# One core, two fused blocks: the first norm's factor applied where results leave PSUM, x loaded in four chunks and turned unnormalised, parameter rows on ScalarE's queue

## The chip, the cores and the metric

The kernel runs on one core of one Trainium2 chip. The metric is the device time of one execution in microseconds (us). Engines: PE (TensorE), ACT (ScalarE), DVE (VectorE), POOL (GpSimd), SP (SyncE, which issues most of the loads).

## The reference

`x` is 1 x 256 x 2048 (fp32). Two blocks follow each other; the change is in the first.

```python
h = rmsnorm(x, norm_mix_pre)                       # x * rsqrt(mean(x*x) + eps) * gain
proj = h @ w_in                                    # 2048 -> 2048 xr | 2048 yr | 2048 q | 256 k | 256 v | 2048 g_rnn | 2048 g_attn
xr = causal_depthwise_conv(xr, conv_w, conv_b)     # width 4
xr = rg_lru(xr, ...)                               # gates by two block matmuls, then a scan over the 256 positions
y_rnn = xr * gelu(yr)
q, k = rope(q), rope(k)
y_att = sliding_window_sink_attention(q, k, v, attn_sinks)
mix = sigmoid(g_rnn) * (y_rnn @ w_rnn_proj) + sigmoid(g_attn) * (y_att @ w_attn_proj)
x = x + rmsnorm(mix @ w_out, norm_mix_post)
# then an MLP with squared relu, and the whole second block (differential attention beside an S5 branch)
```

## The kernel before

**Work.** Every large product is done in fp32 by three matmuls: a weight tile is split into a rounded high part (`w_hi`, ACT, L639) and a low remainder (`w_lo`, DVE, L1079), the activations likewise (`h_hi`, `h_lo`). A *unit* is 512 output columns over all 2048 rows of a weight matrix: eight *subgroups* of 256 rows, each 512 KB of weights, 2 k-tiles, 12 matmuls of 512 columns (24 of 256 where the result is wanted feature-major). The weights of a subgroup pass through a ring of four buffers: SP loads `raw` (L362), ACT writes `w_hi`, DVE writes `w_lo`, PE multiplies. `split_hi` of subgroup g waits until PE has done all subgroups up to g-4; the load of subgroup g waits until DVE has split g-4. `LEAD` is 3: the loop index j of `steps` splits subgroup j+3 of the unit, so the last three turns of a unit prepare the next one. Everything else an engine does is hung between two such splits, as `hooks` by turn number. Each engine's order is written out by hand, and engines meet at semaphores.

**Order of units.** k and v (one unit, `U_KV`); then q and xr alternately, four of each; four units of yr; then 16 units of the mix, and so on. Results go to `acc[0]` and `acc[1]` in turn.

**Start.** SP issues x as one load of 2 MB, then 12 loads of parameter rows into `stg` (L353), then weights. When all 12 have landed PE transposes the two row tiles, and ACT copies them out as columns (`pt1`, `pt2`). Meanwhile ACT squares x (L664), DVE makes the mean square (L1109), POOL the factor `rstd` (L468). Then, for each of four chunks of 512 columns, in turn: ACT scales x by `rstd` into `stg` (L677), PE transposes it (L1745), ACT writes `h_hi` with the gain (L657), DVE `h_lo` (L1098). All four chunks use the same PSUM tile, so one chunk's turning waits for the one before. After POOL's first factor come its loads of gate weights: `load_rg(0)` at once, `load_rg(1)` when the last chunk has been scaled.

**Side work in the first units.** DVE: `rotary_angles`, `cosines_and_lambda`, `softplus`; ACT: `rotary_sines`, `exponentials`, each a hook in the k/v unit. Behind that unit ACT copies v out and DVE rotates k (L1204 and what follows).

**xr, yr and the recurrence.** At the first turn after an xr unit ACT copies `acc[0]` to `slab_d` (`xr_out`, L752), where POOL's convolution reads it. At the end of each yr unit ACT applies gelu straight from PSUM (L812), after it has waited for the convolution of that chunk. Beside yr unit c+1 runs the recurrence of chunk c, in turns of the same splits: PE's gate matmuls `rg(c)` (L1835), ACT `gates` (turn 2), `decays` (turn 3), `root` (turn 4), `y_high` (L772, turn 7); DVE `decay` (turn 3), `states` (turn 5, with the scan L1296), `y_product` (L1302, turn 6), `y_low` (L1307, turn 7).

The code that the change touches, with the line numbers of the profile:

Of the kernel before, what the change touches and what calls it, by code (L numbers as in the profile page):

```python
# [94 lines left out]
def griffin_block_then_ssm_block(nc, a, inv_freq, out):  # L95
    with ExitStack() as ctx:
# [107 lines left out]
        y_hi_ready = sem("y_hi_ready")  # L204
# [134 lines left out]
        def _(sp):  # L339
            x_in = a["x"][0].rearrange("(t p) d -> p t d", p=P)  # L340
            x_view = slab_i[:, :, :].rearrange("p (t k) c -> p t (k c)", t=TT)
            sp.dma_start(x_view, x_in).then_inc(x_landed, 16)
            for rows, tile in ((FIRST_ROWS, 0), (SECOND_ROWS, 1)):
                at = 0
                for name, n in rows:
                    src = a[name]
                    if name == "conv_w":
                        src = src[0].rearrange("w (r c) -> (w r) c", c=P)
                    elif len(src.shape) == 3:
                        src = src[0].rearrange("(r g) s -> r (g s)", g=2)  # L350
# [21 lines left out]
            unit(w_in, slice(o_k, o_k + NC), U_KV * S)  # L372
# [46 lines left out]
        def _(pool):  # L419
# [46 lines left out]
            for n in range(5):  # L466
                pool.wait_ge(ms_ready, n + 1)
                pool.tensor_tensor(small[:, 6:8], small[:, 4:6], neg_half[:, 0:2], ALU.pow).then_inc(rstd_ready, 1)  # L468
                if n == 0:
# [41 lines left out]
                    pool.wait_ge(stg_ready, NH)  # L511
# [115 lines left out]
        def _(act):  # L627
# [34 lines left out]
            act.wait_ge(x_landed, 16)  # L662
            for t in range(TT):
                ins = nc.scalar.activation(slab_d[:, 8 * t:8 * t + 8, :].rearrange("p k c -> p (k c)"), x_tok[:, t, :], ACT.Square,  # L664
                                           accum_out=ssq[:, t, 0:1])
            ins.then_inc(sq_ready, 1)

            act.wait_ge(pt_ready, 1)
            nc.scalar.activation(pt1[:, :], tps[:, 0:P], ACT.Copy)
            nc.scalar.activation(pt2[:, :], tps[:, P:2 * P], ACT.Copy).then_inc(cols_ready, 1)  # L670

            def h_chunk(c, t0, col):

                if c:
                    act.wait_ge(tps_ready, t0 + c)
                for t in range(TT):
                    ins = nc.scalar.activation(stg[:, t, :], x_tok[:, t, c * NC:(c + 1) * NC], ACT.Copy,  # L677
                                               scale=rstd[:, t:t + 1])
                ins.then_inc(stg_ready, 1)
                evac_hi(h_hi[:, c * QPC:(c + 1) * QPC, :], t0 + c + 1, col[:, c * QPC:(c + 1) * QPC])  # L680

            def first_unit(t0, const, col, hooks=None):

                for c in range(NH):
                    if c >= 2:
                        steps(None, 0, const, hooks, c - 1, start=c - 2)
                    h_chunk(c, t0, col)
                steps(None, 0, const, hooks, start=2)
# [13 lines left out]
            for j in range(LEAD):  # L702
                split_hi(None, 0, 0, j)


            act.wait_ge(rstd_ready, 1)
            first_unit(0, U_KV * S, pt1[:, COL1["norm_mix_pre"]:COL1["norm_mix_pre"] + KT],
                       {3: [rotary_sines], 5: [exponentials]})
            unit_over(None, 0, U_KV * S)
            nc.scalar.activation(v_tok[:, :, :], tok(acc[0])[:, :, SEQ:2 * SEQ], ACT.Copy).then_inc(v_ready, 1)  # L710
# [38 lines left out]
            def xr_out(i, c):  # L749
                unit_over(i, 2 * S, (U_QX + 1 + 2 * c) * S)  # L750
                settle()
                nc.scalar.activation(slab_d[:, span(i, QPC, QPC * c, QPC), :], feat(acc[0]), ACT.Copy).then_inc(acc_free[0], 1)  # L752

# [4 lines left out]
            steps(None, 0, U_QX * S, {5: [k_copy]})  # L758
            with act.Fori(0, NH - 1) as i:
                beside_xr, beside_q = attention(i, 0)  # L760
                steps(i, 2 * S, (U_QX + 1) * S, beside_xr)
                beside_q[0] = [lambda: xr_out(i, 0)] + beside_q.get(0, [])
# [3 lines left out]
            beside_yr[0] = [lambda: xr_out(None, NH - 1)] + beside_yr.get(0, [])  # L766
# [47 lines left out]


            def mix_unit(i, c, n, hooks=None):
                u = U_MIX + 4 * c + n
                steps(i, 4 * S, u * S, hooks)
                if n % 2 == 0:
# [5 lines left out]
                    nc.scalar.activation(tmp[:, :, :], tok(acc[u % 2]), ACT.Tanh, scale=0.5).then_inc(acc_free[u % 2], 1)  # L825
# [28 lines left out]

            def x_high(c, t0, col):


                act.wait_ge(tps_ready, t0 + c + 1)
                for b in range(QPC):
                    at = c * QPC + b  # L860
                    ins = nc.scalar.activation(h_hi[:, at, :], x_bank(c, b), ACT.Copy, scale=col[:, at:at + 1])
                ins.then_inc(tps_hi, 1)

            def x_squares(c, first_x):
                act.wait_ge(x_new, first_x + c + 1)
                for t in range(TT):
                    ins = nc.scalar.activation(e_tok[:, t, c * NC:(c + 1) * NC], x_tok[:, t, c * NC:(c + 1) * NC],
                                               ACT.Square, accum_out=ssq[:, t, c:c + 1])
                if c == NH - 1:
                    ins.then_inc(sq_ready, 1)  # L870
# [57 lines left out]
            act.wait_ge(row_ready, 1)  # L928
            nc.scalar.activation(row[:, :], side[0][:, 0:SEQ], ACT.Copy).then_inc(row_copied, 1)
# [143 lines left out]
        def _(dve):  # L1073
# [46 lines left out]
            mean_square(1, 1)  # L1120
            for j in range(LEAD):
                split_lo(None, 0, 0, j)

            def first_unit(hi_index, const, col, hooks=None):

                for c in range(NH):
                    if c >= 2:
                        steps(None, 0, const, hooks, c - 1, start=c - 2)
                    at = slice(c * QPC, (c + 1) * QPC)
                    evac_lo(h_hi[:, at, :], h_lo[:, at, :], hi_index + c, col[:, at])  # L1130
                steps(None, 0, const, hooks, start=2)
# [893 lines left out]
```

## Time and profile before

| | us |
|---|---|
| median of 3 runs | 2401.95 (2401.73 to 2402.02) |
| the profiled execution, its own time | 2403.9 |
| the profiled execution, its span | 2402.2 |
| PE busy in the span | 2269.6 (94%) |
| DVE / ACT / POOL busy | 1463.5 (61%) / 1192.6 (50%) / 457.7 (19%) |
| mean granted TensorE clock | 0.982 of full |

A timeline row reads: start and length in us, engine and line, operation, output from input, shapes, how many were merged; in brackets the idle time just before it and what ended it. The text uses *subgroup* numbers counted from the k/v unit's first: 0 to 7 are k/v, 8 to 15 the first q unit.

### The profile page before, as it was taken

What the parts mean: (1) busy time and instruction counts of PE and PEld (TensorE: products, weight loads), DVE (VectorE), ACT (ScalarE), POOL (GpSimd) and SP (SyncE); (2) the same over time, 40 slices, a digit from 0 to 9 for tenths busy, and PEclk for the clock granted to TensorE, in tenths of its full rate; (3) what the DMA queues carried; (4) which work ended last, traced back from release to release, by engine and by line L of the source; (5) the groups of instructions that cost most, each with busy time, mean ns of one, the idle gap of its engine ahead of it and who ended that gap; (6) DMA issues with size and microseconds to landing.
All of it is one profiled execution on the core that took longest, in us unless ns stands there. A gap on an engine that the chain in (4) does not pass through costs nothing.

```text
span 2402.2 us, 33351 instructions
## 1 busy us (share of the span) xinstructions
PE 2269.6 (94%) x11622; PEld 1902.4 (79%) x11622; DVE 1463.5 (61%) x1634; ACT 1192.6 (50%) x1804; POOL 457.7 (19%) x460
## 2 busy tenths in 40 slices
PE   4999999999999979999999999989999898989999
PEld 3888988788888768888888888869866686767887
DVE  3656669644554565555555555565998966665554
ACT  5455556644444445555555555554444444453443
POOL 2011385000000101211221121110656620100000
PEclk9999999999999989999999999999999999999999
DMA  6544444566666836666666666655555544445665
GB/s 184 176 149 144 145 123 150 172 189 193 190 188 195 261 117 198 200 207 198 198 206 196 200 206 196 199 172 176 171 171 172 179 149 141 147 133 169 183 193 165
DMA packets 214167, 426.41 MB, mean 178 GB/s; under 512 B 13984, under 2 KB 14272, under 8 KB 213312
## 3 DMA queue, kind: packets, MB, share of 16 engines
q1 hardware_dynamic: 206336, 398.64, 54.2%
q0 software_dynamic: 7744, 26.62, 3.4%
q8 instruction: 54, 0.88, 0.1%
q14 instruction: 33, 0.27, 0.0%
HBM read 414.71 MB, written 10.49 MB: 177 GB/s over the span
## 4 chain that ended last, share of the span: by engine, by line
PE 73%; DVE 11%; issue 8%; POOL 3%; ACT 3%; DMA 1%; SPq 0%; DVEq 0%; ACTq 0%; POOLq 0%
PE acc L1730 20%; PE acc L1732 20%; PE acc L1731 20%; DVE w_lo L1079 3%; PE acc L1722 3%; PE acc L1724 3%; PE acc L1725 3%; PE tps L1745 1%; POOL slab_f_f L567 1%; ACT w_hi L639 1%; DMA raw<-in_w_out_dram 1%; DVE k_t L1531 1%; POOL slab_f_f L568 1%; PE sides L1785 1%; PE tps L1803 1%
## 5 line engine op out<-in xcount | busy, mean ns | idle before, releaser
L1079 DVE TENSOR_TENSOR w_lo<-raw,w_hi 128x1024 fp32r<-128x1024 f32 x752 | 967.2, 1293 | 780.1 <-ACT w_hi L639 775.3
L639 ACT ACTIVATE w_hi<-raw 128x1024 fp32r<-128x1024 f32 x752 | 793.0, 1059 | 933.9 <-PE acc L1732 768.9
L1730 PE MATMUL acc<-w_hi,h_hi 128*128 128x512 f32 x1440 | 578.9, 402 | 20.5 <-DVE w_lo L1079 8.3
L1731 PE MATMUL acc<-w_lo,h_hi 128*128 128x512 f32 x1440 | 566.8, 394 | 0.0
L1732 PE MATMUL acc<-w_hi,h_lo 128*128 128x512 f32 x1440 | 566.4, 393 | 0.0
L1730 PEld LDWEIGHTS acc<-w_hi,h_hi 128*128 128x128 f32 x1440 | 274.5, 191 | 92.9 <-issue 23.7
L1732 PEld LDWEIGHTS acc<-w_hi,h_lo 128*128 128x128 f32 x1440 | 274.1, 190 | 59.1
L1731 PEld LDWEIGHTS acc<-w_lo,h_hi 128*128 128x128 f32 x1440 | 274.9, 191 | 54.1
L1730 PE MATMUL acc<-w_hi,slab_dg_r 128*128 128x512 f32 x768 | 300.2, 391 | 3.2 <-DVE w_lo L1079 3.2
L1732 PE MATMUL acc<-w_hi,slab_dg_r 128*128 128x512 f32 x768 | 299.5, 390 | 0.0
L1731 PE MATMUL acc<-w_lo,slab_dg_r 128*128 128x512 f32 x768 | 299.4, 390 | 0.0
L1722 PE MATMUL acc<-h_hi,w_hi 128*128 128x256 f32 x768 | 223.7, 291 | 8.9 <-DVE w_lo L1079 8.9
L1724 PE MATMUL acc<-h_lo,w_hi 128*128 128x256 f32 x768 | 219.2, 285 | 0.0
L1725 PE MATMUL acc<-h_hi,w_lo 128*128 128x256 f32 x768 | 219.1, 285 | 0.0
L1730 PEld LDWEIGHTS acc<-w_hi,slab_dg_r 128*128 128x128 f32 x768 | 144.5, 188 | 33.3 <-issue 3.5
L1732 PEld LDWEIGHTS acc<-w_hi,slab_dg_r 128*128 128x128 f32 x768 | 144.6, 188 | 30.2
L1731 PEld LDWEIGHTS acc<-w_lo,slab_dg_r 128*128 128x128 f32 x768 | 144.6, 188 | 30.0
L1722 PEld LDWEIGHTS acc<-h_hi,w_hi 128*128 128x128 f32 x768 | 149.0, 194 | 15.8 <-DVE w_lo L1079 10.0
L1724 PEld LDWEIGHTS acc<-h_lo,w_hi 128*128 128x128 f32 x768 | 149.3, 194 | 0.2
L1725 PEld LDWEIGHTS acc<-h_hi,w_lo 128*128 128x128 f32 x768 | 149.0, 194 | 0.0
L462 POOL DMA_DIRECT2D trig_scratch<-tmp x32 | 18.8, 589 | 447.3 <-DVE tmp L1454 433.2
L1730 PE MATMUL acc<-w_hi,slab_f_r 128*128 128x512 f32 x256 | 100.4, 392 | 0.0
(374 smaller groups left out, 2439.5 us busy)
## 6 DMA issues: line engine op xcount, KB each, us to landing
raw<-in_w_in_dram SPq DMA_DIRECT2D x328, 512.0 KB, 3.8
raw<-in_w_mlp_up_dram SPq DMA_DIRECT2D x128, 512.0 KB, 3.7
raw<-in_w_mlp_down_dram SPq DMA_DIRECT2D x128, 512.0 KB, 4.6
raw<-in_w_out_dram SPq DMA_DIRECT2D x64, 512.0 KB, 4.6
raw<-in_w_rnn_proj_dram SPq DMA_DIRECT2D x32, 512.0 KB, 3.9
raw<-in_w_attn_proj_dram SPq DMA_DIRECT2D x32, 512.0 KB, 4.6
trig_scratch<-tmp POOLq DMA_DIRECT2D x32, 256.0 KB, 4.0
raw<-in_w_proj_ssm_dram SPq DMA_DIRECT2D x16, 512.0 KB, 5.5
```

The costliest lines, as they stand in the source:

```text
L567: pool.tensor_tensor(xs[n % 4][:, 0, :], t2[:, 0, :], t1[:, 1, :], ALU.subtract).then_inc(state_ready, 1)
L568: pool.tensor_tensor(xs[n % 4][:, 1, :], t2[:, 1, :], t1[:, 0, :], ALU.add).then_inc(state_ready, 1)
L639: nc.scalar.activation(w_hi[:, j % RING], raw[:, j % RING], ACT.Copy).then_inc(hi_ready, 1)
L1079: V.tensor_tensor(w_lo[:, j % RING], raw[:, j % RING], w_hi[:, j % RING].bitcast(F32), ALU.subtract)\
L1531: chain.mark(V.tensor_tensor_scan(t1[:, 0, :], decay, t1[:, 0, :], 0.0, ALU.mult, ALU.add))
L1722: T.matmul(o, wh[:, c], hi[:, k, :], start=first and m % 2 == 0, stop=False, skip_group_check=True)
L1724: T.matmul(o, wh[:, c], lo[:, k, :], start=False, stop=False, skip_group_check=True)
L1725: ins = T.matmul(o, wl[:, c], hi[:, k, :], start=False, stop=last, skip_group_check=True)
L1730: T.matmul(o, hi[:, k, c], wh, start=first, stop=False)
L1731: T.matmul(o, hi[:, k, c], wl, start=False, stop=False)
L1732: ins = T.matmul(o, lo[:, k, c], wh, start=False, stop=last)
L1745: ins = T.transpose(tps[:, b * SEQ + t * P:b * SEQ + (t + 1) * P], stg[:, t, b * P:(b + 1) * P], ident[:, :])
```

## The change

x is loaded in four column chunks, with the weight loads of subgroups 0 to 2 between them. The parameter rows are issued by ACT, the five that are needed first counted apart from the other seven; the second tile is turned after subgroup 2. x is transposed as it is (`turn_x`, in `tps` and `sides` by turns), `h_hi` and `h_lo` get the gain only. The squares are taken beside the k/v unit (turns 1 to 4), the mean square at DVE's turn 5. `rstd` then enters where the results leave PSUM: in the v copy, in the cosines and sines (so in q and k), in the tanh scale of the mix gates, and, as a row over the features made by PE and copied by ACT (`row`), in the outputs of xr and yr. Those two are now multiplied by DVE; gelu follows on ACT from SBUF at turn 0 of the next unit. `exponentials` and `softplus` move to the first q unit; POOL's first `load_rg` comes with the later `rstd`.

```diff
@@ SP
-            sp.dma_start(x_view, x_in).then_inc(x_landed, 16)
-            for rows, tile in ((FIRST_ROWS, 0), (SECOND_ROWS, 1)):
...
-            unit(w_in, slice(o_k, o_k + NC), U_KV * S)
+            for c in range(NH):
+                at = slice(c * NC, (c + 1) * NC)
+                sp.dma_start(x_view[:, :, at], x_in[:, :, at]).then_inc(x_landed[c], 16)
+                if c < LEAD:
+                    load(w_in, slice(o_k, o_k + NC), 2 * c, U_KV * S + c, c)
+            for s in range(LEAD, S):
+                load(w_in, slice(o_k, o_k + NC), 2 * s, U_KV * S + s, s)
@@ POOL
-                    pool.wait_ge(stg_ready, NH)
+                    pool.wait_ge(tps_ready, NH)
                     load_rg(1)
@@ ACT
+            for rows, tile in ((FIRST_ROWS, 0), (SECOND_ROWS, 1)):
...
+                    act.dma_start(stg[at:at + n, tile, 0:P], src).then_inc(rows_landed[tile], 16)
...
+            pt_copy_(0)
+            act.wait_ge(cols_ready, 1)
+            x_high(0, 0, mix_gain)
+            split_hi(None, 0, 0, 0)
+            split_hi(None, 0, 0, 1)
+            x_high(1, 0, mix_gain)
+            split_hi(None, 0, 0, 2)
+            hooks = {s: [lambda c=s - 1: x_squares(c, None)] for s in range(1, 5)}
+            hooks[2].append(lambda: pt_copy_(1))
+            hooks[5] = [rotary_sines]
+            for c in range(2, NH):
+                x_high(c, 0, mix_gain)
+                steps(None, 0, U_KV * S, hooks, c - 1, start=c - 2)
+            steps(None, 0, U_KV * S, hooks, start=2)
+            unit_over(None, 0, U_KV * S)
             act.wait_ge(rstd_ready, 1)
...
+            for t in range(TT):
+                ins = nc.scalar.activation(v_tok[:, t, :], tok(acc[0])[:, t, SEQ:2 * SEQ], ACT.Copy, scale=rstd[:, t:t + 1])
...
-            steps(None, 0, U_QX * S, {5: [k_copy]})
+            steps(None, 0, U_QX * S, {1: [exponentials], 3: [lambda: row_copy(1)], 5: [k_copy]})
...
+            def gelu(c):
+                u = U_YR + c
+                act.wait_ge(acc_free[u % 2], u // 2 + 1)
+                at = slice(c * QPC, (c + 1) * QPC)
+                nc.scalar.activation(slab_d[:, at, :], slab_d[:, at, :], ACT.Gelu_apprx_tanh).then_inc(gelu_ready, 1)
...
-                return {2: [lambda: gates(c)], 3: [lambda: decays(c)], 4: [lambda: root(c)], 7: [lambda: y_high(c)]}
+                return {0: [lambda: gelu(c)], 2: [lambda: gates(c)], 3: [lambda: decays(c)], 4: [lambda: root(c)], 7: [lambda: y_high(c)]}
...
-                act.wait_ge(conv_ready, c + 1)
-                unit_over(None, 0, u * S)
-                nc.scalar.activation(slab_d[:, c * QPC:(c + 1) * QPC, :], feat(acc[u % 2]), ACT.Gelu_apprx_tanh)\
-                    .then_inc(acc_free[u % 2], 1)
@@ DVE
+                dve.wait_ge(rstd_ready, 1)
+                chain.mark(V.tensor_scalar(half_rstd, rstd, 0.5, None, ALU.mult))
+                for t in range(TT):
+                    for b in (cosb, sinb):
+                        chain.mark(V.tensor_scalar(b[:, t, :], b[:, t, :], rstd[:, t:t + 1], None, ALU.mult))
...
+            x_low(0, H_X, mix_gain)
+            split_lo(None, 0, 0, 0)
+            split_lo(None, 0, 0, 1)
+            x_low(1, H_X, mix_gain)
+            split_lo(None, 0, 0, 2)
+            hooks = {3: [rotary_angles], 5: [lambda: mean_square(NH, 1)], 6: [cosines_and_lambda]}
...
+            def xr_out(i, c):
+                unit_over(i, 2 * S, (U_QX + 1 + 2 * c) * S)
+                rows_ = row[:, :].unsqueeze(1).broadcast_to([P, QPC, SEQ])
+                dve.wait_ge(row_copied, 1)
+                V.tensor_tensor(slab_d[:, span(i, QPC, QPC * c, QPC), :], feat(acc[0]), rows_, ALU.mult).then_inc(acc_free[0], 1)
+
+            steps(None, 0, U_QX * S, {2: [softplus]})
...
+                dve.wait_ge(conv_ready, c + 1)
+                unit_over(None, 0, u * S)
+                rows_ = row[:, :].unsqueeze(1).broadcast_to([P, QPC, SEQ])
+                V.tensor_tensor(slab_d[:, c * QPC:(c + 1) * QPC, :], feat(acc[u % 2]), rows_, ALU.mult).then_inc(acc_free[u % 2], 1)
@@ PE
+            turn_rows(0)
+            for c in range(2):
+                turn_x(c, 0, None)
+            unit(None, 0, U_KV * S, 0, U_KV, h_hi, h_lo, hooks={4: [lambda: turn_rows(1)]},
+                 before={2 * c: [lambda c=c: x_as_it_comes(c, 0, None)] for c in range(NH)})
+            pe.wait_ge(cols_ready, 2)
...
-            unit(None, 0, U_QX * S, 0, U_QX, h_hi, h_lo, hooks={9: [lambda: turn(None, 0, T_K)]})
+            unit(None, 0, U_QX * S, 0, U_QX, h_hi, h_lo, hooks={5: [lambda: rstd_row(1)], 9: [lambda: turn(None, 0, T_K)]})
```

`turn_x(c)` waits for chunk c of x and, from the third chunk on, for the PSUM tile of two chunks before; `x_as_it_comes(c)`, ahead of subgroup 2c, waits for `h_lo` of chunk c and then turns chunk c+2. `turn_rows(n)` turns one tile of parameter rows, `pt_copy_(n)` copies it out. `x_high` and `x_low` are `h_hi` and `h_lo` of one chunk, `x_squares(c)` two squares of 128 x 512 with their sums.

## Rows read from the trace of the kernel before

**Rows 1.** The page: the chain that ended last, by engine

```profile
PE 73%; DVE 11%; issue 8%; POOL 3%; ACT 3%; DMA 1%; SPq 0%; DVEq 0%; ACTq 0%; POOLq 0%
```

**Rows 2.** PE's waits, 0 to 120 us: line waited for, us in total, times, longest

```profile
PE tps L1770 <- DMA stg<-in_ssm_lambda_im_dram: 14.9, 1, 14.9
PE tps L1745 <- ACT stg L677: 8.2, 1, 8.2
PE acc L1730 <- DVE w_lo L1079: 6.6, 5, 1.8
```

**Rows 3.** Timeline of all engines, 0 to 60 us

```profile
0.87 0.44 SPq L342 DMA_DIRECT2D slab_i_f<-in_x_dram  x1
...
8.20 48.09 SPq L362 DMA_DIRECT2D raw<-in_w_in_dram  x12
...
23.80 1.94 PE L1745 MATMUL tps<-ident,stg 128*128 128x128 f32 x8 [8.21 <-ACT stg L677]
25.78 1.57 ACT L657 ACTIVATE h_hi<-tps,pt 128x256 fp32r<-128x256 f32 x4 [2.12 <-PE tps L1745]
...
27.38 1.66 DVE L1098 SCALAR_TENSOR_TENSOR h_lo<-tps,pt,h_hi 128x256 fp32r<-128x256 f32 x4 [3.69 <-ACT h_hi L657]
...
30.78 0.78 PE L1730 MATMUL acc<-w_hi,h_hi 128*128 128x512 f32 x1
```

**Rows 4.** Timeline of DVE, 30 to 110 us

```profile
86.18 0.69 DVE L1204 TENSOR_TENSOR tmp<-acc,cosb 128x512 f32<-128x512 f32 x1 [0.34 <-PE acc L1732]
```

**Rows 5.** Timeline of ACT, 470 to 486 us

```profile
475.37 1.06 ACT L639 ACTIVATE w_hi<-raw 128x1024 fp32r<-128x1024 f32 x1 [1.66 <-PE acc L1732]
```

**Rows 6.** Busy time by window: us, each engine's busy time, PE clock, DMA share, GB/s

```profile
120.00:285.00 165.00, 165.00 (x1182) 142.88 (x1181) 99.94 (x151) 94.45 (x203) 26.84 (x29) 1.00 0.49 150
```

**Rows 7.** DMA issues, 0 to 60 us: KB each, median us from issue to landing

```profile
raw<-in_w_in_dram SPq DMA_DIRECT2D x12, 512.0 KB, 5.7
slab_i_f<-in_x_dram SPq DMA_DIRECT2D x1, 2048.0 KB, 9.8
...
slab_h_f<-in_lambda_k_dram POOLq DMA_DIRECT2D x2, 32.0 KB, 8.5
```

**Rows 8.** The page: DMA issues of the whole span, the same columns

```profile
raw<-in_w_in_dram SPq DMA_DIRECT2D x328, 512.0 KB, 3.8
```

**Rows 9.** Timeline of ACT, 355 to 363 us

```profile
356.59 1.06 ACT L772 ACTIVATE slab_e_r<-tmp 128x1024 fp32r<-128x1024 f32 x1 [13.16 <-DVE tmp L1302]
357.67 1.28 ACT L812 ACT_TABLE_LOAD   x1
358.96 1.02 ACT L812 ACTIVATE slab_dg_f<-acc 128x1024 f32<-128x1024 f32 x1
359.88 2.94 ACT L639 ACTIVATE w_hi<-raw 128x1024 fp32r<-128x1024 f32 x3
```

**Rows 10.** Timeline of DVE, 385 to 398 us

```profile
391.41 3.40 DVE L1079 TENSOR_TENSOR w_lo<-raw,w_hi 128x1024 fp32r<-128x1024 f32 x1
394.73 2.90 DVE L1307 TENSOR_TENSOR slab_i_r<-tmp,slab_e_r 128x1024 fp32r<-128x1024 f32 x1
```

**Rows 11.** The tile `sides`, 86 to 330 us: ns min/median/max of each

```profile
L1240 DVE SCALAR_TENSOR_TENSOR slab_i_f<-sides,mask x16: 927/950/959, 97.9 to 295.0; 128x768 f32<-128x768 f32 x16
```

**Rows 12.** Timeline of ACT, 30 to 110 us

```profile
47.99 1.28 ACT L692 ACT_TABLE_LOAD   x1
53.14 0.26 ACT L692 ACTIVATE sinb<-pi 128x64 f32<-128x64 f32 x1 [3.87 <-DVE pi L1118]
```

**Rows 13.** Timeline of PE, 395 to 430 us

```profile
400.95 0.58 PE L1722 MATMUL acc<-h_hi,w_hi 128*128 128x256 f32 x1 [2.95 <-DVE w_lo L1079]
...
419.69 3.61 PE L1835 MATMUL tps<-stg,slab_e_f 128*128 128x256 f32 x16
```

**Rows 14.** Busy time by window, around that row

```profile
400.00:405.00 5.00, 4.05 (x21) 4.05 (x22) 4.30 (x4) 4.97 (x8) 0.00 (x0) 0.66 0.55 177
```

**Rows 15.** Timeline of DVE, 395 to 486 us

```profile
410.65 2.35 DVE L1079 TENSOR_TENSOR w_lo<-raw,w_hi 128x1024 fp32r<-128x1024 f32 x2
```

More of the change, by code:

```diff
@@ L672, in h_chunk @@
-            def h_chunk(c, t0, col):
-                if c:
-                    act.wait_ge(tps_ready, t0 + c)
-                for t in range(TT):
[L677 to L688, printed above, removed]
+            for rows, tile in ((FIRST_ROWS, 0), (SECOND_ROWS, 1)):
+                at = 0
+                for name, n in rows:
+                    src = a[name]
+                    if name == "conv_w":
+                        src = src[0].rearrange("w (r c) -> (w r) c", c=P)
+                    elif len(src.shape) == 3:
+                        src = src[0].rearrange("(r g) s -> r (g s)", g=2)
+                    else:
+                        src = src[0].rearrange("(r c) -> r c", c=P)
+                    act.dma_start(stg[at:at + n, tile, 0:P], src).then_inc(rows_landed[tile], 16)
+                    at += n
@@ new lines, in pt_copy_, with x_high @@
+            def pt_copy_(n):
+                act.wait_ge(pt_ready, n + 1)
+                nc.scalar.activation((pt1, pt2)[n][:, :], acc[1][:, n * NC:n * NC + P], ACT.Copy).then_inc(cols_ready, 1)
+            def x_high(c, t0, col):
+                act.wait_ge(tps_ready, t0 + c + 1)
+                for b in range(QPC):
+                    at = c * QPC + b
+                    ins = nc.scalar.activation(h_hi[:, at, :], x_bank(c, b), ACT.Copy, scale=col[:, at:at + 1])
+                ins.then_inc(tps_hi, 1)
@@ L927, in _ @@
             steps(None, 0, G_U, start=2)
-            act.wait_ge(row_ready, 1)
-            nc.scalar.activation(row[:, :], side[0][:, 0:SEQ], ACT.Copy).then_inc(row_copied, 1)
+            row_copy(2)
             def b_blocks(c):
@@ L1768, in _, with turn_rows, x_as_it_comes, rstd_row @@
             pe.wait_ge(ident_ready, 1)
-            pe.wait_ge(rows_landed, 16 * (len(FIRST_ROWS) + len(SECOND_ROWS)))
-            T.transpose(tps[:, 0:P], stg[:, 0, 0:P], ident[:, :])
-            T.transpose(tps[:, P:2 * P], stg[:, 1, 0:P], ident[:, :]).then_inc(pt_ready, 1)
-            pe.wait_ge(cols_ready, 1)
-            turn(None, 0, 0)
-            unit(None, 0, U_KV * S, 0, U_KV, h_hi, h_lo, before=chunks_as_they_come(0))
+            def turn_rows(n):
+                pe.wait_ge(rows_landed[n], 16 * len((FIRST_ROWS, SECOND_ROWS)[n]))
+                T.transpose(acc[1][:, n * NC:n * NC + P], stg[:, n, 0:P], ident[:, :]).then_inc(pt_ready, 1)
+            def x_as_it_comes(c, t0, first_x):
+                pe.wait_ge(tps_free, t0 + c + 1)
+                if c < NH - 2:
+                    turn_x(c + 2, t0, first_x)
+            def rstd_row(index):
+                pe.wait_ge(rstd_ready, index)
+                for t in range(TT):
+                    ins = T.matmul(side[0][:, t * P:(t + 1) * P], rstd[:, t:t + 1].broadcast_to([P, P]), ident[:, :],
+                                   start=True, stop=True)
+                ins.then_inc(row_ready, 1)
+            turn_rows(0)
[4 more added lines that the diff above has]
+            pe.wait_ge(cols_ready, 2)
             def attention(i, c):
@@ L1875, in _ @@
                 turn_x(c, T_N2, NH)
[L1877 to L1891 removed]
+            unit(None, 0, G_U, 0, U_U, h_hi, h_lo, by_feature=True, hooks={14: [lambda: rstd_row(5)]},
+                 before={2 * c: [lambda c=c: x_as_it_comes(c, T_N2, NH)] for c in range(NH)})
             def turn_b(c):
```

140 lines of the change are left out of this document (48 added, 92 removed).

## The prediction

> **What bounds the kernel now.** I read the page first, for the chain that ended last: nearly three quarters of it is PE [rows 1], so a microsecond saved pays only where PE stands still. Then PE's waits over the first 120 us. The first matmul for the k/v unit starts at 30.78 us [rows 3]. Before it PE waits 14.9 us for the last of the parameter rows and 8.2 us for ACT's scaled first chunk [rows 2]; after it, it waits five times for DVE's low parts, 6.6 us in all. From the windows the reader is to see that this is over then: between 120 and 285 us PE is busy for 165.0 of 165 us [rows 6]. The first q unit ends at 86.1 us, where DVE's rotation is released [rows 4]. So 86.1 us is the date to beat: what comes before it is latency and stalls, what comes behind it is PE's own work until the recurrence beside the yr units. There DVE and ACT set the pace: PE waits for `w_lo` again, once for 2.95 us [rows 13], and the order of the two engines' lists matters more than their sums.
>
> **The start, term by term.** Call R the time at which the five first parameter rows have landed. In the new order PE turns them (one tile, about 0.45 by its share of the eight transposes that follow, plus their latency), then turns chunk 0 of x as it came: 1.94 us; ACT writes `h_hi`: 1.57; DVE `h_lo`: 1.66; PE turns chunk 2, which stands ahead of subgroup 0 in its order: 1.94 [all rows 3]. With some 0.05 us for each handover the first subgroup starts at R + 7.7 us. In the old order two more things stood in this chain, the squares with the factor and the scaling by it. Both leave it. The second chunk's turning lies beside ACT's and DVE's work on the first.
>
> From there a subgroup takes 2.72 us: ACT's `w_hi` waits 1.66 us for PE and works 1.06, over and over [rows 5]. Sixteen subgroups are 43.5 us. What PE does between them until the first q unit ends: turning chunk 3 0.8, the second parameter tile 0.25, the new factor row 0.4 (two 128-column products, both estimates from the 1.94 us for eight), turning k 0.8, and 0.75 for the first subgroups, where PE was still slow (its first matmul took 0.78 us [rows 3]; an estimate). Sum 46.5, so the q unit ends at R + 54.2 us, if PE never waits. I laid the three lists out in order with the durations of the trace to see whether it does: `h_hi` and `h_lo` of chunk c are done well before subgroup 2c, the four squares (1.2 us a chunk on ACT, an estimate from `y_high`'s 1.06 for 1024 columns [rows 9] and the reading of two sums) push `w_hi`, but the tightest subgroups, 4 and 7, still find `w_lo` about 1.5 us early. The five old stalls came from DVE's and ACT's small work in the same unit (angles, cosines, softplus), and now softplus lies in the q unit behind subgroup 13, with PE two subgroups away. The five added DVE operations (cosines, sines, half factor; under 1 us) go into that slack, as do the v copy in two parts and POOL's two `load_rg`, now 2 MB in one go beside the weights: a load may take up to 7 us there before its subgroup feels it. If that cover were gone, each would cost its own length.
>
> So the gain is 86.1 - 54.2 - R = 31.9 - R.
>
> **R.** No DMA in this trace is issued by ACT. SP's first 13 took from 0.87 to 8.20 us, 0.56 each [rows 3]: the fifth row is issued at 3.7 us if ACT does as SP. From issue to landing, the bounds are 3.8 us, the median over all the k/v, q and other `w_in` loads [rows 8], and 8.5 us, a small load of POOL's in the thick of the x transfer [rows 7]. I take 5.7, what SP's loads of the first 60 us needed [rows 7], since it is the hardware queue's own price in a busy stretch. R = 9.4, with ends 7.5 and 12.2. Chunk 0 of x (a quarter of what took 9.8 us [rows 7]) is there by then, chunks 1 and 2 too, with the loads between them: all 4 MB of x and weights at the rate of x (2 MB in 9.8 us with the latency in it) are wanted only by R + 13. Gain 31.9 - 9.4 = 22.5, ends 24.4 and 19.7.
>
> The Trainium skill, "DMA: Bandwidth & Descriptors", in its sections "Anatomy of one DMA" and "Queues, rings and completion order", gives about 2 us of fixed cost and has each DMA engine serve the queue rows in turn, packet by packet, so that rows on ACT's own queue would not stand behind x. By it R would be near 5.8, the second chunk of x would bind instead, and the gain would be some 2 us above mine; the trace speaks against so short a landing, with 3.8 us as the whole span's median [rows 8].
>
> **xr beside the attention.** DVE takes over four outputs of xr. A PSUM operation of 128 x 768 with an SBUF operand took 0.95 us, 0.927 to 0.959 in 16 runs, POOL busy or not [rows 11]; for 1024 columns I take 1.2 us. It stands at turn 0, ahead of `y_low` of the attention's first pair, and behind it a `soft`. PE wants that result 3 k-tiles into the unit, 4.2 us, and has it by about 3.2 to 4.0. In three of four units I cost this at nothing. In the fourth POOL's convolution runs beside it and slows what DVE does with two SBUF operands; I put 1 us, ends 0 and 3.
>
> **The recurrence.** This is where the change gives back. Take T, the end of `y_product`. Before, ACT went on at once: `y_high` 1.06, table load 1.28, gelu 1.02, three `w_hi` 2.94 [rows 9]; the gates began at T + 6.2. Now gelu needs DVE's product with the row, and that stands at the end of DVE's unit: `w_lo` 3.3 and `y_low` 2.85, both slow because POOL's convolution runs (undisturbed `w_lo` is 1.18 [rows 15]), then the product 1.2 [rows 10]. Then gelu 1.0 and two `w_hi` 1.9: T + 10.2. So 4.0 us later per round. The table load I put at nothing: where ACT has a single wait, it stands ahead of the wait (47.99, the sine itself at 53.14 [rows 12]), and gelu now has one wait where it had two. If it stays behind the wait: + 1.3 per round.
>
> The round is closed: gates, decays, DVE's `decay`, `states`, scan, `y_product`. It sets the pace in two of the three boundaries between yr units; in the first one PE's `rg(0)` is later than either, and at the last one POOL is done and PE's `rg(3)` holds ACT. Two rounds are 8.0 us on `w_lo` of the last subgroup of the fourth yr unit. PE had slack there: that `w_lo` was ready at 411.8 [rows 15], and PE took it at 419.69 - 2.72 - 2.88 = 414.1 [rows 13]. 8.0 - 2.3 = 5.7; laid out in order it comes to 5.5. All behind it moves by that much. The wait for the convolution, which goes from ACT to DVE with the next unit's `w_lo` queued behind it, is over 2 us or more before it is asked in each unit. Ends: 4 us, and 10.7 if the product is slowed to 2.9 like its neighbours.
>
> After 457 us I find nothing: the mix gates' tanh in two halves (about 0.35 us more, eight times) ends far ahead of PE's next need of `acc`.
>
> **Sum.** -22.5 + 0.5 (handovers that the layout misses) + 1 + 5.5 = -15.5 us. On the profiled execution's 2403.9 that is 2388.4; the medians lie 1.95 lower: 2401.95 - 15.5 = 2386.5.
>
> **Rivals.**
> 1. *The rows don't get past x.* If their completion comes only with the 4 MB of x and first weights, at x's rate (2.4 MB with the small loads in about 9 us) R = 0.9 + 16.5 = 17. Or ACT's issues take twice SP's time, and the copy of the columns, queued behind all twelve, starts near 14. Gain 15 to 18: -8 to -11, 2391 to 2394. For: before, the last row landed at 14.9 us [rows 2]. Against: it was then issued last behind 2 MB on one queue. The skill's same page, "Rules for kernel authors", says that spreading DMAs over queues saves issue time only, which is this rival's side.
> 2. *The recurrence costs double.* Table load behind the wait and a slow product: 13.3 us by the same layout. -22.5 + 0.5 + 1 + 13.3 = -7.7, 2394.3. For: `y_low` at 2.90 us [rows 10] where `w_lo`, of the same shape, took 1.18 undisturbed. Against: rows 11 and 12.
> 3. *More.* R at its early end of 7.5, and PE's slack swallows more of the two rounds: -24.4 + 2.4 = -22, 2380.
> 4. *Slower.* DVE and ACT hand each other every step. If all three boundaries pay the slow `w_lo`, `y_low`, product, table load and two `w_hi` (13.2 against 6.2, 7.0 each), 21 us; and the longer stalls drop PE's clock: after its 2.95 us of idleness the granted clock was 0.66 over 5 us [rows 14], part of it at 1.2 instead of 2.4 GHz: 0.34 x 5 = 1.7 us lost; three of these, 5. With 1 for xr, 27 against a gain of 22: +5, 2407. It decides from 7.3 us per boundary. Against it: at the first boundary PE's `rg(0)` is later than the chain.
>
> **How the numbers follow.** Forecast 0.60, rival 1 0.12, rival 2 0.14, rival 3 0.06, rival 4 0.04, and 0.04 for no change by a sum of misses. Within 0.2% is 4.8 us, about what a measurement here tells from nothing. The first four are faster by more: 0.92. Same 0.04, slower 0.04. The forecast alone spans 2381 to 2392 (gain 24.4 or 19.7, loss 5 to 10). The range takes in most of rivals 1 to 3: 2379 to 2395.
>
> **What would show it.** Right: PE's first matmul of k/v near 17 us, its wait for parameter rows 9 to 10 us, the first q unit over near 64 us (now 86.1), no wait of PE for `w_lo` above 1 us in between. In the yr units `L812`'s successor begins 4 to 5 us after DVE's `y_low`, the fourth yr unit ends 5 to 6 us less early than the third q unit does, and PE waits for `w_lo` ahead of the last subgroup of the third or fourth yr unit. Wrong: rows landing after 13 us; DVE's product above 2 us; a table load behind DVE's product; a stall of `turn_p` beside xr.

## The result, and the profile after

The changed kernel is faster: 2389.74 us median of 6 runs (2387.20 to 2394.49) against 2402.68 (2401.73 to 2406.93, 6 runs) before, ratio 0.9944, 95% interval 0.9933 to 0.9954. That is 12.9 us less where 15.5 were forecast (2386.5 us), inside the range of 2379 to 2395. The profiled execution took 2391.41 us, its span is 2389.7.

PE's waits from 0 to 120 us (line waited for, us in total, times, longest), where [rows 2] stood before:

```profile
PE acc L1780 <- DMA stg<-in_b_rg_x_dram: 9.6, 1, 9.6
PE tps L1772 <- DMA slab_i_f<-in_x_dram: 1.9, 1, 1.9
```

Both waits for ACT and the five for `w_lo` are gone. The chain that replaced them, from the timeline of all engines, 0 to 18 us, against [rows 3]:

```profile
3.51 0.49 ACTq L666 DMA_DIRECT2D stg<-in_b_rg_x_dram  x1
...
9.57 0.45 PE L1780 MATMUL acc<-ident,stg 128*128 128x128 f32 x1 [9.57 <-DMA stg<-in_b_rg_x_dram]
...
11.83 1.57 ACT L679 ACTIVATE h_hi<-tps,pt 128x256 fp32r<-128x256 f32 x4 [1.50 <-PE tps L1772]
...
13.51 1.66 DVE L1121 SCALAR_TENSOR_TENSOR h_lo<-tps,pt,h_hi 128x256 fp32r<-128x256 f32 x4 [13.51 <-ACT h_hi L679]
...
15.37 1.94 PE L1772 MATMUL tps<-ident,slab_i_f 128*128 128x128 f32 x8 [1.94 <-DMA slab_i_f<-in_x_dram]
16.96 0.78 PE L1743 MATMUL acc<-w_hi,h_hi 128*128 128x512 f32 x1
```

The reader is to see R = 9.57 (9.4 was predicted), the first k/v matmul at 16.96 (before 30.78), and one row that the prediction had not priced: ahead of it PE turns chunk 2, and it waited for that chunk's load.

The first q unit ends, seen at DVE's rotation, at 64.18 us (86.18 in [rows 4]): 22.0 gained.

```profile
64.18 0.69 DVE L1202 TENSOR_TENSOR tmp<-acc,cosb 128x512 f32<-128x512 f32 x1 [0.34 <-PE acc L1745]
```

The attention keeps all of it: the gates of chunk 0 start at 305.86, before at 327.79. Then the recurrence gives back. ACT's timeline, 330 to 346 us, where [rows 9] stood:

```profile
334.64 1.06 ACT L784 ACTIVATE slab_e_r<-tmp 128x1024 fp32r<-128x1024 f32 x1 [13.15 <-DVE tmp L1319]
335.60 1.04 ACT L633 ACTIVATE w_hi<-raw 128x1024 fp32r<-128x1024 f32 x1
336.66 1.28 ACT L819 ACT_TABLE_LOAD   x1
341.90 1.06 ACT L819 ACTIVATE slab_dg_f<-slab_dg_f 128x1024 f32<-128x1024 f32 x1 [3.96 <-DVE slab_dg_f L1335]
342.87 1.99 ACT L633 ACTIVATE w_hi<-raw 128x1024 fp32r<-128x1024 f32 x2
344.76 1.54 ACT L791 ACTIVATE slab_dg_f<-tps,half_b 128x256 f32<-128x256 f32 x4
```

and what it waits for, in DVE's:

```profile
334.53 3.39 DVE L1076 TENSOR_TENSOR w_lo<-raw,w_hi 128x1024 fp32r<-128x1024 f32 x1
337.84 2.90 DVE L1324 TENSOR_TENSOR slab_i_r<-tmp,slab_e_r 128x1024 fp32r<-128x1024 f32 x1
340.66 1.21 DVE L1335 TENSOR_TENSOR slab_dg_f<-acc,t_low 128x1024 f32<-128x1024 f32 x1
```

The table is loaded ahead of the wait, and the product takes 1.21 us while POOL's convolution runs: both as forecast. The gates start 10.1 us after `y_product` is over, before 6.2. The chunks' gates follow each other at 38.90 and 38.89 us (34.93 and 34.93 before), so two rounds lose 7.9. The third distance is 32.3 us against 32.9. From the gates of chunk 0 to the table load of the mix's first tanh it is 133.67 us against 126.33: 7.3 lost.

### The profile page after: what moved, and what is told of

Same layout as the page of the kernel before. It is cut to its first block, busy times and chain, and to the rows that moved or that the text cites. A ratio compares the mean times of both kernels' runs of the same rounds, so it can differ in the third digit from the quotient of the medians.

```text
span 2389.7 us, 33386 instructions
## 1 busy us (share of the span) xinstructions
PE 2274.0 (95%) x11626; PEld 1907.8 (80%) x11626; DVE 1469.2 (61%) x1648; ACT 1187.0 (50%) x1814; POOL 456.0 (19%) x460
## 4 chain that ended last, share of the span: by engine, by line
PE 73%; DVE 11%; issue 8%; POOL 3%; ACT 3%; DMA 1%; SPq 0%; DVEq 0%; ACTq 0%; POOLq 0%
PE acc L1743 21%; PE acc L1745 20%; PE acc L1744 20%; PE acc L1735 3%; DVE w_lo L1076 3%; PE acc L1737 3%; PE acc L1738 3%; PE tps L1758 1%; POOL slab_f_f L561 1%; ACT w_hi L633 1%; DMA raw<-in_w_out_dram 1%; DVE k_t L1544 1%; POOL slab_f_f L562 1%; PE sides L1811 1%; PE tps L1829 1%
```

## The experiments

Two theories of the start (the rows' queue, or x itself, sets R) and two of the loss (the *order* of DVE's list, or the *sum* of DVE's work) were set against each other. Two executions of one kernel differ by up to 9.5 us (e4), so the marks of each profile stand beside the medians. The medians come from four series of runs, in which the old kernel's own median was 2402.68, 2403.40, 2403.96 and 2403.20. "Rows landed" is R (in e8 and e11 the gain rows alone); "half pace" is what PE lost at its start, explained with e9 to e11; "to tanh" runs from the q unit's end to the table load of the mix's first tanh; "behind" is the rest of the span. The diffs are shortened to what matters; "..." marks what is left out.

| run | median, us | rows landed | first matmul | half pace | q unit over | to tanh | behind |
|---|---|---|---|---|---|---|---|
| before | 2402.68 | 14.92 (all 12) | 30.78 | 0.81 | 86.18 | 367.9 | 1948.1 |
| changed | 2389.74 | 9.57 | 16.96 | 1.03 | 64.18 | 375.4 | 1950.2 |
| changed, again | 2390.34 | 10.04 | 16.83 | 0.11 | 63.06 | 375.2 | 1948.1 |
| e1 rows behind x | 2401.22 | 21.55 | 28.33 | 1.57 | 76.06 | 375.3 | 1950.8 |
| e2 all rows | 2394.94 | 15.64 | 22.43 | 0.11 | 68.70 | 375.3 | 1947.7 |
| e3 x in one load | 2390.75 | 12.17 | 19.50 | 1.07 | 67.58 | 373.8 | 1947.3 |
| e8 gain rows alone | 2391.47 | 4.33 | 18.48 | 2.12 | 66.93 | 373.8 | 1947.0 |
| e4 no yr factor | 2382.43 | 9.96 | 18.55 | 1.51 | 66.22 | 369.0 | 1949.4 |
| e5 product behind y | 2383.04 | 9.87 | 17.21 | 2.14 | 65.55 | 367.8 | 1948.7 |
| e6 product ahead | 2383.36 | 9.92 | 19.08 | 0.63 | 65.88 | 370.3 | 1945.8 |
| e7 product twice | 2391.19 | 9.73 | 18.31 | 0.93 | 65.44 | 377.9 | 1944.5 |
| e9 turned later | 2386.28 | 9.96 | 16.84 | 1.41 | 65.36 | 368.0 | 1950.3 |
| e10 weights first | 2384.28 | 9.80 | 16.68 | 2.61 | 66.37 | 369.2 | 1950.4 |
| e11 gain rows too | 2380.59 | 4.47 | 14.33 | 2.71 | 64.27 | 369.1 | 1950.3 |

**e1, rows on SP's queue again.**

```diff
-  act.dma_start(stg[at:at + n, tile, 0:P], src)   # all 12, ACT
+  sp.dma_start(stg[at:at + n, tile, 0:P], src)    # behind chunk 3 of x, ahead of the weights of subgroup 3
```

> The changed kernel with its 12 parameter rows issued by SP again, behind all four chunks of x and the first three weight loads; ACT issues nothing. My theory (a queue of its own carries the rows past x): SP needs about 0.56 us for each issue, so the fifth row is issued near 8 us instead of 3.9 and lands 5.7 us later at the earliest (13.7), at x's rate with 3.5 MB ahead of it at the latest (17). R goes from 9.6 to 13.7 to 17, the first k/v matmul from 17.0 to 21 to 24, and the whole time up by 4 to 7.5 us against the changed kernel. Rival (the rows do not bind, chunk 0 of x does): first matmul at most 1 us later, time within 1 us.

DMA issue (KB, us to landing) and PE's timeline:

```profile
stg<-in_b_rg_x_dram SPq DMA_DIRECT2D x1, 8.0 KB, 13.6
```

```profile
21.55 0.45 PE L1779 MATMUL acc<-ident,stg 128*128 128x128 f32 x1 [21.55 <-DMA stg<-in_b_rg_x_dram]
```

Issued at 7.81 instead of 3.51, the fifth row landed 13.6 us later, where ACT's queue took 5.9. R rose by 12.0, the first matmul by 11.4, the q unit by 11.9 and the median by 11.5 us (ratio to before 0.9992, interval 0.9983 to 1.0001). My theory's direction held and its size failed, upwards: with the rows in this place nearly the whole gain is gone. Two things differ here, the queue and the place behind 3.5 MB, where the old kernel had the rows behind 2 MB only. The five rows on SP's queue ahead of x were not tried, so it is not shown that it takes a second queue. The Trainium skill, "DMA: Bandwidth & Descriptors", in "Rules for kernel authors", has it, of bandwidth, that spreading loads over queues saves issue time only. Of the 12.0 us on this row 4.3 were issue time; 7.7 were not, against a queue with 3.5 MB ahead. The same page's packet-by-packet turns between queues fit the direction. Its fixed cost of about 2 us, given there for loads issued by GpSimd, is not what these rows took (3.5 us for the first, 5.9 to 6.2 for the next four).

**e2, all rows waited for.**

```diff
-  pe.wait_ge(rows_landed[n], ...)
+  for m in range(2): pe.wait_ge(rows_landed[m], ...)
```

> The changed kernel, but the first turning waits for all 12 rows instead of five. The twelfth is issued at 7.1 us; with the 5.9 to 6.2 us that the later ones of the first five took, it lands at 13.2 to 13.6. My theory: R 13.4 instead of 9.6, first k/v matmul near 20.8, the time up by 3.8 us. Rival (the second tile's rows are small and the queue is clear by then, or x binds anyway): less than 1.5 us.

R is 15.64, where I expected 13.4: the last row, issued at 7.67, took 8 us. The first matmul comes 5.5 us later, the q unit ends 4.5 us later, the median is 5.2 higher (0.9971, interval 0.9961 to 0.9981). Waiting for five alone is worth about 5 of the 6.1 us by which R differs.

**e3, x in one load.**

```diff
-  for c in range(NH): sp.dma_start(x_view[:, :, at], x_in[:, :, at]).then_inc(x_landed[c], 16); load(...)
+  sp.dma_start(x_view, x_in).then_inc(x_landed[0], 16); then the three loads
```

> The changed kernel with x as one load of 2 MB again, the first three weight loads behind it. My theory: x lands at 10.7 us as before, the first turning starts there instead of at 9.8, and the first weight buffer (wanted by ACT at 13.3) is there in time or 1 to 2 us late: time up by 1 us, ends 0 and 3. Rival (it is the chunking that lets the work start early): up by 5 us or more, since x and the weights share the rate and the whole of x is then ahead of the first weights.

The median moved by 1.0 us, which its interval (0.9939 to 0.9966) doesn't tell from nothing. The way was another than I wrote: the rows, on their own queue, landed at 12.17 instead of 9.57; only the loads on SP's queue differ, and why the rows took longer is not shown. The q unit ended 3.4 us later. The median hides a part of that, as the recurrence happened to be 1.5 us shorter in this profile (explained below). The chunks matter by 1 to 3.4 us, not by 5.

**e8, gain rows alone.**

```diff
-  T.transpose(acc[1][:, 0:P], stg[:, 0, 0:P], ident)       # all five landed
+  T.transpose(acc[1][:, 0:16], stg[0:16, 0, 0:P], ident)   # norm_mix_pre landed; the rest turned after subgroup 2
```

> The changed kernel, but only the 16 rows of the norm's gain are waited for and turned first; the rest of both tiles is turned after subgroup 2. They were issued at 0.9 us and landed 3.5 us later, so R falls from 9.6 to 4.4 and chunk 0 of x binds. The naive reading of my formula (gain is 31.9 minus R) gives 3 to 5 us less. My theory now: the raw weights of subgroup 2 landed at 19.9 us, their low part is ready at 22.2, and PE took it at 22.4; so the first matmul comes 3 to 4 us earlier, PE stalls ahead of subgroup 2 for as much, and the q unit ends at most 0.3 us earlier: time within 0.5 us of the changed kernel. Rival (that load comes earlier too, when nothing waits for rows): 3 us less.

```profile
4.33 0.26 PE L1785 MATMUL acc<-ident,stg 16*128 16x16 f32 x1 [4.33 <-DMA stg<-in_norm_mix_pre_dram]
5.89 1.97 PE L1776 MATMUL tps<-ident,slab_i_f 128*128 128x128 f32 x8 [1.30 <-DMA slab_i_f<-in_x_dram]
10.26 1.97 PE L1776 MATMUL sides<-ident,slab_i_f 128*128 128x128 f32 x8 [2.40 <-DMA slab_i_f<-in_x_dram]
16.89 1.94 PE L1776 MATMUL tps<-ident,slab_i_f 128*128 128x128 f32 x8 [4.67 <-DMA slab_i_f<-in_x_dram]
18.48 0.78 PE L1747 MATMUL acc<-w_hi,h_hi 128*128 128x512 f32 x1
```

No gain, as expected (the median is 1.7 higher, the q unit 2.7 us later), and not for the reason that I gave. Not the weights of subgroup 2 but chunk 2 of x is the date: it landed at 16.9, and it stands ahead of the first product. "Gain = 31.9 - R" holds down to R of about 9.5 and no further.

**e4, no yr factor.**

```diff
+  act: nc.scalar.activation(slab_d[:, ...], feat(acc[u % 2]), Gelu_apprx_tanh)   # end of each yr unit, from PSUM
-  dve: V.tensor_tensor(slab_d[:, ...], feat(acc[u % 2]), rows_, mult)
```

> The changed kernel with gelu taken straight from PSUM at the end of each yr unit, as before, and DVE's product with the row taken out there: the first norm's factor is left out of yr. My theory (the order of the lists: gelu stands behind the slow splits of DVE, 4 us in each of two rounds, less 2.3 us of slack, and 1.5 us for the halved clock after the longer stall): 7.3 us less than the changed kernel, gates of chunk 3 at about 408.6 instead of 416.0. Rival (DVE is simply the fuller engine and pays for its own four products, 1.2 us each): 2.4 to 4.8 us less.

This kernel leaves the first norm's factor out of yr. It takes 7.3 us less by the medians (ratio to before 0.9903, interval 0.9889 to 0.9917), 6.3 less to tanh. The rounds are 34.94 and 34.94 us again, as before.

**e5 and e6, the same work in another place.**

```diff
   # DVE, turn 6
-  6: [y_product(c)]                         # the product with the row stood behind turn 7
+  6: [y_product(c), yr_out(c + 1)]          # e5
+  6: [yr_out(c + 1), y_product(c)]          # e6, and ACT: gelu(c + 1) ahead of y_high(c) at turn 7
```

> The changed kernel with the same work, but DVE's product of yr units 2 to 4 with the row stands right behind y_product (turn 6) instead of behind the last split and y_low; PE is through with the unit by then (its next gate matmuls began before DVE's scan was over). ACT's order is not touched. Theory of order: gelu finds its input when y_high and one w_hi are done, the gates come 6.2 us after y_product again instead of 10.2, and 5.5 to 7.5 us come back. Theory of DVE's sum: nothing comes back, as DVE has as much to do: within 1 us.

> As the run before it, but DVE's product stands ahead of y_product, and ACT's gelu ahead of y_high, in the 13 us in which ACT waits for y_product. Theory of order: the closed round gets 1.2 us longer by the product and 2.3 us shorter by table load and gelu, so 1.1 us per round less than the run before; with two rounds that set the pace, 7 to 9.5 us less than the changed kernel, the best of all. Theory of DVE's sum: within 1 us of the changed kernel. If PE is the later one again at every boundary, no more than the run before gives.

ACT's timeline of e5:

```profile
335.94 1.06 ACT L784 ACTIVATE slab_e_r<-tmp 128x1024 fp32r<-128x1024 f32 x1 [13.15 <-DVE tmp L1319]
...
337.97 1.28 ACT L819 ACT_TABLE_LOAD   x1
339.26 1.06 ACT L819 ACTIVATE slab_dg_f<-slab_dg_f 128x1024 f32<-128x1024 f32 x1
...
342.12 1.55 ACT L791 ACTIVATE slab_dg_f<-tps,half_b 128x256 f32<-128x256 f32 x4
```

Gelu waits for nothing, and the gates come 6.2 us after `y_product`, as in the old kernel. To tanh it is 367.8 us, the old kernel's 367.9, with all of DVE's added work still there. The median is 2383.04 (0.9901, interval 0.9889 to 0.9914): 6.7 us below the changed kernel. So the loss was the place of one instruction in DVE's list, and DVE's sum cost nothing.

e6 is as fast as e5 by the medians (0.9907, interval 0.9894 to 0.9920), not faster, and to tanh it takes 2.5 us more. Its first round took 32.59 us, 2.4 less than e5's, but its second 40.14. DVE's timeline of e5 and then of e6 in that round, and POOL's of e6:

```profile
360.32 4.50 DVE L1313 TENSOR_TENSOR_SCAN tmp<-tmp,slab_dg_f 128x256 f32<-128x256 f32 x4
```

```profile
360.50 9.86 DVE L1313 TENSOR_TENSOR_SCAN tmp<-tmp,slab_dg_f 128x256 f32<-128x256 f32 x4
```

```profile
359.48 2.73 POOL L496 TENSOR_TENSOR slab_e_f<-slab_dg_f,pt 128x1020 f32<-128x1020 f32 x1
362.29 2.62 POOL L498 TENSOR_TENSOR stg<-stg,slab_e_f 128x1020 f32<-128x1020 f32 x1
364.99 2.14 POOL L496 TENSOR_TENSOR slab_e_f<-slab_dg_f,pt 128x1016 f32<-128x1016 f32 x1
```

In e5 and in the changed kernel three of the four scans begin beside POOL's one-input `L491` and take 0.68 to 0.93 us each, the fourth lies beside the two-input `L496` and takes 2.3. In e6 the scans began no earlier than in e5, since ACT had waited for weights and for PE on the way; but POOL had begun its convolution 0.9 us earlier and was through with `L491` at 359.4 instead of 362.1. So all four scans lay beside two-input operations, and each took 2.3 to 2.8 us. That cost 5.4 us, more than the first round had given.

**e7, product twice.**

> The changed kernel with DVE's product of yr with the row done twice, one behind the other (1.3 us more with the handover). Theory of order: only the two rounds that set the pace pay, and no slack is left: 2.6 us more. Theory of DVE's sum: four products, and the next unit's splits pushed in each: 5 us more. If the product has slack behind it: nothing.

The rounds are 40.18 and 40.17 us, 1.28 longer each, and 2.5 longer to tanh: two rounds pay, without slack. The median rose by 1.5, which the ratios don't tell from nothing (0.9945 against 0.9944).

**e9, e10, e11, the start once more, on e5.**

```diff
-  before={0: h_lo(0) done, turn_x(2);  2: h_lo(1) done, turn_x(3);  4: ...}
+  before={0: h_lo(0) done;  2: h_lo(1) done, turn_x(2);  3: turn_x(3);  4: ...}    # e9
-  SP: x0 w0 x1 w1 x2 w2 x3 w3
+  SP: x0 w0 x1 w1 w2 x2 w3 x3     # e10, and e11 with e8's gain rows
```

> The run e5 (DVE's product behind y_product) with chunk 2 of x turned ahead of subgroup 2 instead of subgroup 0, chunk 3 ahead of subgroup 3, and ACT's and DVE's work on them one split later. In the profiles so far PE turned chunk 2 between 15.4 and 17.5 us, four times of six only when it had landed, with the first k/v matmul behind it at 17.0 to 19.1. My theory (that landing is the second date of the start, right behind the rows): the first matmul comes near 16.4 whenever chunk 2 lands, the first q unit ends at 63.7 to 64.3 instead of 65.5 (the middle of the runs with this start), and the time is 1 to 2 us below e5. Rival (the raw weights of subgroup 2, which land at 19.9 to 20.2, bind instead): q unit as in e5, no difference.

> The run before it, and SP issues the weights of subgroups 2 and 3 ahead of chunks 2 and 3 of x. My theory: the low part of subgroup 2 is ready near 22.3 in the run before it and PE asks for it near 23, so nothing: within 1 us of it. Rival (weights bind from subgroup 2 on): the low part of subgroup 2 comes 2 us earlier and the q unit ends up to 2 us earlier.

> The run before it, and only the norm's 16 gain rows are waited for at the start, as in e8, where that gave nothing because chunk 2 of x bound. With chunk 2 out of the way my theory is that the early rows pay now: ACT is free of its twelve issues and the table load at 9.1 us, the first matmul comes near 13.8, the q unit ends near 61.5, and the time is 2 to 2.5 us below the run before it. Rival (the transfer rate of the first 20 us is the bound whatever the order): within 1 us of it.

e9's first matmul comes at 16.84 without waiting for chunk 2, but its q unit ends at 65.36 against e5's 65.55, and e10's at 66.37. The theory of two dates missed a third, PE's pace. The windows of e10 and then of the changed kernel's second profile (us, each engine's busy time with its instructions, PE clock, DMA share, GB/s):

```profile
18.00:20.00 2.00, 2.00 (x6) 1.52 (x5) 2.00 (x5) 0.00 (x0) 0.00 (x0) 1.00 0.94 322
20.00:22.00 2.00, 2.00 (x6) 1.52 (x6) 0.37 (x1) 0.79 (x1) 0.00 (x0) 1.00 1.07 383
```

```profile
18.00:20.00 2.00, 2.00 (x11) 1.64 (x10) 1.49 (x4) 0.00 (x0) 0.00 (x0) 1.00 0.91 290
20.00:22.00 2.00, 2.00 (x11) 1.65 (x10) 0.58 (x1) 1.67 (x3) 0.00 (x0) 1.00 1.00 384
```

PE has no gap in any of them, and yet does 6 matmuls in 2 us in e10 and 11 in the other. The clock column is no guide in e10: the trace has no clock record before 22.08 us there, and the view prints 1.00 where there is none. In e1, e6, e7 and e9 the records reach back to the slow matmuls, and show the lower level, 1.2 GHz. e9:

```profile
17.00:19.00 2.00, 2.00 (x5) 1.61 (x6) 2.00 (x5) 0.13 (x1) 0.00 (x0) 0.50 0.86 242
```

There PE had stood idle from 13.4 to 16.84 us. Matmuls of 512 columns came 0.43 us apart there, and 0.23 from 19.9 us on, where the record is back at 1.00. The same half pace is seen in the others, with the change at 19.12 in the first profile, 21.62 in e5, 22.24 in e10; that their missing records would show 0.50 is inferred from the spacing alone. The lost time (span of the slow matmuls less 0.227 us for each) is the column "half pace". The old kernel has it too, 0.81 us.

Take it off, and from the first matmul to the q unit's end it is 46.1 to 46.2 us in all six profiles with the changed kernel's start (changed twice, e4 to e7), and 47.1 to 47.2 in e9 to e11, which now turn chunk 2 inside that stretch. e10's median is 2.0 below e9's while its q unit ends 1.0 later, so no effect of the order of weights and chunks is shown. e11 has its first matmul 2.4 us earlier than e10, and its median is 3.7 lower; but 13 of its matmuls ran at half pace. Its ratio to before is 0.9899 (0.9883 to 0.9914), e5's 0.9901: the intervals lie on each other, so nothing is shown for it over e5. e9's median is 3.2 above e5's with the same marks up to tanh, where 1 to 2 below was expected; the difference lies behind, and I have no cause for it.

**e12, the changed kernel again.**

> The changed kernel itself once more, for the scatter of its start: its profiled run had the q unit over at 64.2 us, and the four runs with the same start 65.4 to 66.2. If the landing of chunk 2 is what scatters, this one shows the q unit over between 64 and 66.5 us, with the first matmul earlier or later by nearly the same, and a median near 2390.

Its median is 2390.34 (0.9930 to 0.9957). The q unit ended at 63.06, a microsecond outside what I expected, and chunk 2 was turned no earlier (15.86 against 15.37). PE was at full pace by then:

```profile
15.86 1.07 PE L1772 MATMUL tps<-ident,slab_i_f 128*128 128x128 f32 x8 [1.96 <-DMA slab_i_f<-in_x_dram]
```

The same eight transposes took 1.94 us in the first profile, and from their start to the first matmul it was 1.59 us there and 0.97 here. So the half pace costs 0.6 us more than its column says where it covers this turning. It, and not chunk 2, puts this start ahead of the first profile's.

## Why the prediction was right, point by point

**The start, 22.0 net of handovers: right in the profile shown, a little high on average.** The profile has 22.0, the six profiles with this start 21.1 (q unit over at 65.06 in the mean, against the one profile of the old kernel). R is 9.57 to 10.04, against 9.4. From the first matmul it is 46.2 plus the half pace of 0.1 to 2.2; I had 46.5 with 0.75 for it. What I had wrong is "chunks 1 and 2 too": chunk 2 is not there by then. It is wanted at R + 5.7 and was turned at 15.4 to 17.5; in five of the six profiles PE waited for it, and the first matmul came 6.8 to 9.2 us after R instead of 7.7. That I counted the whole 4 MB as wanted only by R + 13 hid it.

**R, and rival 1.** In e1 the rows behind x landed at 21.55, later than rival 1's 17, and only 1.5 us of gain was left by the medians, where I gave it 8 to 11. On ACT's queue, with nothing large on it, they landed at 9.6 to 10.0.

**xr beside the attention, +1: nothing.** From the q unit's end to the first gates it is 241.6 to 241.7 us in every profile of a changed kernel, and 241.6 before. A slow product beside POOL didn't come; xr was not tried by itself.

**The recurrence, +5.5: the mechanism right, the size 7.3.** The 4.0 per round is right (3.97 and 3.96), the two rounds are right, the table load ahead of its wait and the product at 1.2 too. The term that was mis-sized is the last, "8.0 - 2.3 = 5.7". The slack of 2.3 us was there: the stall ends 5.7 to 5.8 us later than the old kernel's PE took up that subgroup, counted from the gates of chunk 0. But the new stall costs more than itself. PE's timeline and windows of the changed kernel:

```profile
397.90 0.58 PE L1735 MATMUL acc<-h_hi,w_hi 128*128 128x256 f32 x1 [3.13 <-DVE w_lo L1076]
```

```profile
398.00:400.00 2.00, 2.00 (x10) 2.00 (x11) 2.00 (x2) 1.27 (x2) 0.00 (x0) 0.50 0.41 66
400.00:402.00 2.00, 2.00 (x14) 2.00 (x14) 1.93 (x3) 0.00 (x0) 0.00 (x0) 0.68 1.00 378
```

After 3.13 us of idleness PE runs at the lower of its two levels, 1.2 GHz, for some 3 us (256 columns every 0.21 us instead of 0.12) and loses 1.5: 5.8 + 1.5 = 7.3. I had read the same in [rows 14], used it in rival 4 alone, and not in the forecast. The old kernel pays it too, after its wait of 2.95 us, but ahead of the slack. e3 and e8 have the same recurrence and show it by its absence:

```profile
401.28 0.39 PE L1734 MATMUL acc<-h_hi,w_hi 128*128 128x256 f32 x1 [1.68 <-DVE w_lo L1075]
```

```profile
400.00:405.00 5.00, 3.72 (x28) 3.59 (x29) 4.93 (x6) 2.66 (x3) 0.00 (x0) 1.00 0.46 145
```

In e3 the last stall was 1.68 us, the clock stayed at 1.00, the last gates came 30.82 us after those before them (32.32 in the changed kernel), and 373.8 to tanh is 5.9 us above the old kernel, near the forecast's term. The stall ends at the same date in both, 92.0 to 92.1 us after the gates of chunk 0; it is shorter in e3 because PE comes to it 1.5 us later, having run at the lower clock behind the stall before it. In the changed kernel the lower clock fell ahead of that stall, from 377.4 to 380.8 us. PE's timeline and windows there, the changed kernel first, then e3:

```profile
382.99 0.39 PE L1735 MATMUL acc<-h_hi,w_hi 128*128 128x256 f32 x1 [1.50 <-DVE w_lo L1076]
383.00:386.00 3.00, 3.00 (x25) 3.00 (x26) 2.21 (x2) 3.00 (x8) 0.00 (x0) 1.00 0.58 165
```

```profile
386.34 0.39 PE L1734 MATMUL acc<-h_hi,w_hi 128*128 128x256 f32 x1 [2.96 <-DVE w_lo L1075]
387.00:390.00 3.00, 3.00 (x16) 3.00 (x16) 1.57 (x2) 3.00 (x10) 0.00 (x0) 0.50 0.75 234
```

e8 goes the way of e3, with 0.62 us of idleness at its last stall. So where the lower clock falls decides: ahead of a stall that is there anyway it costs nothing, behind the last one 1.5 us. Why it falls otherwise in e3 and e8 than in the profiles with 32.3 us is open.

**Rival 2** (product slowed) did not come: 1.21 to 1.23 us in every yr unit. The Trainium skill's "SBUF — State Buffer", in "Who interferes with whom", has it that VectorE contends with GpSimd when it has two inputs in SBUF. The trace agrees: this product has one in PSUM and takes 1.21, `w_lo` beside it 3.39. But the scans, with two in SBUF, took only 0.68 to 0.93 us beside POOL's `L491`, which reads SBUF, and 0.67 with POOL idle. **Rival 3** wanted R at 7.5 and more slack; neither was there. **Rival 4** needed 7.3 us at three boundaries; two paid 4.0, and the first paid nothing.

**Behind the yr units, nothing: right.** This stretch is 1944.5 to 1950.8 us in the 13 profiles of changed kernels, 1948.5 in the mean, 1948.1 before. The first profile's 1950.2 is scatter, its repetition has 1948.1. One part of it is seen: between 700 and 830 us PE waits for `w_lo`, at its longest 2.2 to 4.2 us, different in each execution (3.2 before).

**Sum by what was measured:** -21.1 + 0 + 7.3 + 0.4 = -13.4, against -12.9 by the medians and -15.5 forecast. That the forecast came this near is in part luck: the 1 us put on xr did not come and covers half of what the recurrence lacked. A small slip in the prediction's bounds, besides: its largest gain with its smallest loss gives 2382 to 2383, not 2381.

## What to carry to other kernels

Small loads on which the first instruction waits must not stand behind large ones; here a queue of their own kept them clear. When that date is mended, ask for the next one at once, here chunk 2 of x, then PE's slow start. Where an operation moves from one engine to another in a closed round of three engines, its place in the new engine's list comes first: behind a slow split and `y_low` it cost 4 us per round, two places earlier nothing. Its length counts only where it stands on the chain (e7, 1.28 us per round). A stall that a change makes longer is to be priced with the clock behind it, in the forecast and not only in a rival, where the old trace shows the lower clock after a stall of that length.

## What the runs showed of the hardware that was not expected

At the start of a kernel matmuls of 512 columns came 0.43 us apart instead of 0.23, for none to 13 of them, and the date of the change differs between executions of one kernel (before 15.86 us in one profile, 19.12 in the other). Where the trace has clock records for this stretch they show 0.50 (e1, e6, e7, e9); where it has none the view prints 1.00, so the spacing is the surer sign. A scan of 128 x 256 on DVE took 0.67 us alone, 0.68 to 0.93 beside POOL's one-input operation and 2.3 to 2.8 beside its two-input ones. In the one profile with x as a single load of 2 MB, rows on another queue landed at 12.2 us, against 9.6 to 10.0 in the seven with four pieces in the same place.
